# High less bias on GpSimd, and the low activations of the upper tiles straight from the bank

## The chip, the cores and the metric

The kernel runs on one core of a Trainium2 chip. A core has five engines that run side by side and wait for one another through semaphores: TensorE (matrix products, PE in the profile, with its weight loads as PEld), VectorE (DVE), ScalarE (ACT), GpSimd (POOL) and SyncE (SP), which here issues the loads. The metric is device time in microseconds, the median of several runs.

## The reference, cut to what matters

The program is two layers of a transformer-like trunk on 256 tokens of 1024 channels. Each layer has four sub-layers (gated feed-forward, a mixer of three branches, cross-attention, feed-forward), and each ends in a layer norm:

```
def layer_norm(x, g, b):
    mu = jnp.mean(xf, -1, keepdims=True)
    var = jnp.mean(jnp.square(xf - mu), -1, keepdims=True)
    return ((xf - mu) * lax.rsqrt(var + LN_EPS) * g + b)

for l in range(DEPTH):
    x = layer_norm(ALPHA * x + 0.5 * swiglu(x, ffn1_wg[l], ffn1_wu[l], ffn1_wd[l]), ln1_g[l], ln1_b[l])
    z = x @ w_in[l]
    ...
    x = layer_norm(ALPHA * x + merged @ mix_w_out[l], ln2_g[l], ln2_b[l])
    x = layer_norm(ALPHA * x + cross_attention(x, mem, xa_wq[l], xa_wkv[l], xa_wo[l]), ln3_g[l], ln3_b[l])
    x = layer_norm(ALPHA * x + 0.5 * swiglu(x, ffn2_wg[l], ffn2_wu[l], ffn2_wd[l]), ln4_g[l], ln4_b[l])
```

The result of each norm is the left operand of the next large product: `w_in` after norm 0, the queries after norm 1, the gate and up weights after norms 2 and 3. The last norm of the second layer is the output and does not go through the code that changes. So that code runs seven times.

## The kernel before, in words

**Products in parts.** TensorE works in float32r, which keeps fewer bits than float32. To hold the accuracy, each operand is split into a high part (rounded to float32r) and a low part (the exact value less the high part, rounded again). A product is then high x high, high x low and low x high.

**Weights.** SyncE loads pieces of 128x1024 into a ring of six (`ring_raw`). ScalarE copies a piece with rounding to `ring_hi`, a ring of three; VectorE subtracts, raw less high, to `ring_lo` (L1718, `lo_to`, 1024 columns a time). Three of the pieces in each layer are subtracted by GpSimd instead (L2444). A slot of `ring_hi` is free again when TensorE has multiplied the piece, so ScalarE, and behind it VectorE, follow TensorE.

**Activations.** `xT[0]` is the high part and `xT[1]` the low part of the normed activations, turned so that channels lie on the partitions: eight tiles of 128 channels x 256 tokens, numbered 0 to 7.

**A norm.** The norm sums up per token (L1732, L1737), GpSimd makes the inverse standard deviation (L2421), and the normed tokens are turned by TensorE into four banks (L850), two channel tiles to a bank. Banks 4 and 5 hold the lower tiles 0 to 3, banks 6 and 7 the upper tiles 4 to 7. What the turned values still need is the norm's gain and bias, which are one number for each channel and so for each partition here. From there two pairs of engines share the work:

- Lower tiles: ScalarE writes the high tiles (bank x gain + bias, rounded), then the same unrounded into `xf`. GpSimd subtracts (L2429), 128x512 at a time, two tiles of one bank.
- Upper tiles: VectorE does all of it. It writes four high tiles (L1755), then what the list `after` holds (in most norms one weight piece, L1718), then for each bank two unrounded tiles into `xf` (L1755 again) and one subtraction of 128x512 (L1769):

```
for b in range(2, 4):
    sl = slice(2 * b, 2 * b + 2)
    st.then(affine(xf, b))
    st.mark(tt(xT[1][:, sl, :], xf[:, sl, :], xT[0][:, sl, :], ALU.subtract), s_xTd)
```

`st.mark` raises a semaphore when the instruction is done; `st.then` also makes the engine wait for it. Each engine works in the order of its program. On VectorE the next work behind this code is the next weight piece. On GpSimd, behind the lower subtractions, norms 0 and 1 have passes of 128x1024 over `x_tok` (L2436, L2437), which scale the residual.

**The first product after a norm.** `first_chunk` takes two weight pieces m = 0 and m = 1. It first does all products of high activations, for m = 0 and then for m = 1 (L775, 32 of them), and then those of the low activations (L786, 16 of them, eight for each piece). Both go over the tiles in the order 4, 5, 6, 7, 0, 1, 2, 3. At L786 it waits for `s_xTd` before tiles 4 and 6 and for `s_xTp` (GpSimd's) before tiles 0 and 2. After norm 1 TensorE has other products to do ahead of `first_chunk`.

All waits in the region are written out by hand in the program; there is no planner.

Of the kernel before, what the change touches and what calls it, by code (L numbers as in the profile page):

```python
# [18 lines left out]
ALU = mybir.AluOpType  # L19
# [7 lines left out]
T = 256  # L27
# [137 lines left out]
def trunk(nc, io, consts, out):  # L165
    with ExitStack() as ctx:
# [17 lines left out]
        def sem(name, n=None):  # L184

            s = nc.alloc_semaphore(name)
            per_layer[s.name] = n
            return s

        def at(s, n):  # L190

            return s, layer[0] * per_layer[s.name] + n
# [19 lines left out]
        def view(region, at, *dims):  # L212

            n = 1
            for d in dims:
                n *= d
            v = region[:, at:at + n]
            if len(dims) == 1:
                return v
            names = "abcd"[:len(dims)]  # L220
            return v.rearrange(f"p ({' '.join(names)}) -> p {' '.join(names)}",
                               **{x: d for x, d in zip(names[1:], dims[1:])})
# [12 lines left out]
        def pc(name, k=0, n=1):  # L235
            a = (PCOL_A if name in PCOL_A else PCOL_B)[name][0]
            return pcol[:, a + k:a + k + n]

        xtok = view(xtok_t, 0, NT, D)
        xT = [view(xT_t, i * ND * T, ND, T) for i in range(2)]  # L240
# [64 lines left out]
        xf = view(work, 6144, ND, T)  # L305
# [44 lines left out]
        def bank(b, *dims):  # L350
            names = "abcd"[:len(dims)]
            if len(dims) <= 1:
                return banks[b][:, :]
            return banks[b][:, :].rearrange(f"p ({' '.join(names)}) -> p {' '.join(names)}",
                                            **{x: d for x, d in zip(names[1:], dims[1:])})
# [43 lines left out]
        s_xhd = sem("xT_hi_from_dve", 8)  # L399
        s_lnx = sem("ln_normalised_dve", 4)  # L400
        s_lnxa = sem("ln_normalised_act", 8)
        s_lnT = sem("ln_turned", 20)
        s_xTa = sem("xT_from_act", 8)
        s_xTd = sem("xT_from_dve", 8)
        s_xg = sem("x_tok_scaled_by_pool", 6)
        s_xgd = sem("x_tok_scaled_by_dve", 10)
# [187 lines left out]
        def done_chunk(eng, kind, j):  # L594

            eng.wait_ge(*at(s_piece, INDEX[(kind, j, 1)] + 1))
# [1107 lines left out]
        def _(dve):  # L1704
            st = Steps(dve, c_dve)
            v = nc.vector
            tt, ts, stt = v.tensor_tensor, v.tensor_scalar, v.scalar_tensor_tensor
# [13 lines left out]
            def ln(n, kind, j, scale, after, within=(), between=(), halfway=()):  # L1721

                if n in (1, 2):
                    dve.wait_ge(*at(s_xg, 4 * n - 2))
                for t in range(NT):
                    for h in range(2):
                        if t == 0 or h == 0:
                            dve.wait_ge(*at(s_acc, 3 * n + 2 * t + h + 1))
                        else:
                            done_chunk(dve, kind, j)  # L1730
                        x = xtok[:, t, 512 * h:512 * h + 512]
                        ins = stt(x, banks[4 + 2 * t + h][:, :], scale, x, ALU.mult, ALU.add)  # L1732
                        if h == 1:
                            st.then(ins, s_lny)
                        else:
                            st.then(ins)
                        st.then(v.bn_stats(stats[t][:, 6 * h:6 * h + 6], x))  # L1737
                    st.then(v.bn_aggr(mv[t], stats[t]))
                    st.mark(ts(vare[t], mv[t][:, 1:2], LNE, None, ALU.add), s_lnv)  # L1739
                    if t == 0:  # L1740
                        for piece in halfway:
                            lo_to(*piece, further=False)
                if n == 3 and layer[0] == L - 1:
                    return
                x = xtok[:, 1, 0:512]
                st.mark(ts(x, x, mv[1][:, 0:1], None, ALU.subtract), s_lnc)
                for piece in within:
                    lo_to(*piece, further=False)
                dve.wait_ge(*at(s_lnr, NT * n + NT))
                x = xtok[:, 1, 512:D]  # L1750
                st.mark(ts(x, x, mv[1][:, 0:1], rstd[1], ALU.subtract, ALU.mult), s_lnx)

                def affine(o, b):
                    for d in (2 * b, 2 * b + 1):
                        ins = ts(o[:, d, :], bank(4 + b, 2, T)[:, d % 2, :], pc(f"ln{n}_g", d), pc(f"ln{n}_b", d),  # L1755
                                 ALU.mult, ALU.add)
                    return ins

                for piece in between:
                    lo_to(*piece, further=False)  # L1760
                for b in range(2, 4):
                    dve.wait_ge(*at(s_lnT, 5 * n + b))
                    st.mark(affine(xT[0], b), s_xhd)
                for piece in after:
                    lo_to(*piece, further=False)
                for b in range(2, 4):
                    sl = slice(2 * b, 2 * b + 2)
                    st.then(affine(xf, b))
                    st.mark(tt(xT[1][:, sl, :], xf[:, sl, :], xT[0][:, sl, :], ALU.subtract), s_xTd)  # L1769

            def add_halves(kind, j, m, o):
                dve.wait_ge(*at(s_piece, INDEX[(kind, j, m)] + 1))
# [50 lines left out]
            for b in (2, 3, 0, 1):  # L1823
# [4 lines left out]
                sl = slice(2 * b, 2 * b + 2)  # L1828
# [193 lines left out]
            for l in range(L):  # L2022
# [81 lines left out]
                for t in range(NW):  # L2104
                    ins = ts(kk[:, t, :], zrw[:, 4 + t, 1:T + 1], pc("k_k", t), None, ALU.mult)
# [11 lines left out]
                for t in range(NW):  # L2117
                    ins = v.tensor_tensor_scan(dec[:, t, :], const("reset"), sw[:, t, :], 0.0, ALU.mult, ALU.add)
# [5 lines left out]
                for t in range(NW):  # L2124
                    ins = ts(rk[:, t, :], ra[:, t, :], pc("k_a", t), omka[:, t:t + 1], ALU.mult, ALU.add)
# [8 lines left out]
                for h in range(2):  # L2134
                    ins = tt(kk[:, 2 * h:2 * h + 2, :], kk[:, 2 * h:2 * h + 2, :], bank(4 + h, 2, T), ALU.mult)
# [16 lines left out]
                for t in range(NW):  # L2152
                    ins = tt(AR[:, t, :, 0, :], kk[:, t, :].rearrange("p (c s) -> p c s", c=NC),
                             eP[:, t, :].rearrange("p (c s) -> p c s", c=NC), ALU.mult)
                st.then(ins)
                dve.wait_ge(*at(s_exp, 3))
                for t in range(NW):
                    ins = tt(AR[:, t, :, 1, :], r_[:, t, :].rearrange("p (c s) -> p c s", c=NC),
                             eC[:, t, :].rearrange("p (c s) -> p c s", c=NC), ALU.mult)
# [3 lines left out]
                for h in range(2):  # L2163
                    ins = tt(bonus[:, 2 * h:2 * h + 2, :], bank(6 + h, 2, T), v_[:, 2 * h:2 * h + 2, :], ALU.mult)
# [140 lines left out]
                for h in range(2):  # L2305
                    ins = stt(yc[:, 2 * h:2 * h + 2, :], bank(4 + h, 2, T), -1.0 / C, yT[:, 2 * h:2 * h + 2, :],
                              ALU.mult, ALU.add)
# [7 lines left out]
                for t in range(NW):  # L2315
                    ins = ts(yc[:, t, :], yc[:, t, :], pc("gn_g", t), pc("gn_b", t), ALU.mult, ALU.add)
# [89 lines left out]
        def _(pool):  # L2406
            st = Steps(pool, c_pool)
            g = nc.gpsimd
            tt = g.tensor_tensor
# [4 lines left out]
            def ln(n, first=None):  # L2414

                final = n == 3 and layer[0] == L - 1
                if first:
                    piece_lo(*first)
                for t in range(NT):
                    pool.wait_ge(*at(s_lnv, NT * n + t + 1))  # L2420
                    st.then(tt(rstd[t], vare[t], NEG_HALF, ALU.pow), s_lnr)  # L2421
                    if t == 0:
                        st.mark(g.tensor_scalar(nbias[0], mv[0][:, 0:1], rstd[0], -1.0, ALU.mult, ALU.mult), s_lnb)
                if final:
                    return
                for b in range(2):
                    pool.wait_ge(*at(s_xTa, 2 * n + b + 1))
                    sl = slice(2 * b, 2 * b + 2)
                    st.mark(tt(xT[1][:, sl, :], xf[:, sl, :], xT[0][:, sl, :], ALU.subtract), s_xTp)  # L2429
                if n >= 2:  # L2430
                    return
                pool.wait_ge(*at(s_lnw, 32 * (n + 1)))
                pool.wait_ge(*at(s_xTd, 2 * n + 2))
                pool.wait_ge(*at(s_lnT, 5 * n + 5))
                for t in range(NT if n else 1):
                    st.then(tt(xtok[:, t, :], xtok[:, t, :], lnbc[:, 0, :], ALU.mult), s_xg)  # L2436
                    st.then(tt(xtok[:, t, :], xtok[:, t, :], lnbc[:, 1, :], ALU.add), s_xg)  # L2437
# [17 lines left out]
            for l in range(L):  # L2455
# [13 lines left out]
                for i in range(2):  # L2469
                    for h in range(2):  # L2470
                        ins = tt(c_bd[i][:, :, 64 * h:64 * h + 64], c_raw[i],
                                 half_c[:, h:h + 1].unsqueeze(2).to_broadcast([P, NW, C]), ALU.mult)
# [4 lines left out]
                for i in range(4):  # L2477
                    a, b = ((frb, fib), (fib, frb), (fr1b, fi1b), (fi1b, fr1b))[i]
# [3 lines left out]
                    for h in range(2):  # L2482
                        dst = b_bd[i].rearrange("p t (s h c) -> p (t s) h c", s=4, h=2)[:, :, h, :]
                        ins = tt(dst, bt_tmp[0], half_s[:, h:h + 1].unsqueeze(2).to_broadcast([P, NS, 16]), ALU.mult)
# [57 lines left out]
```

## Time and profile before

| | |
|---|---|
| time, median of 3 runs | 1641.42 us (1639.29 to 1641.63) |
| profiled execution: its time / its span | 1640.61 us / 1638.7 us |
| TensorE busy | 1589.4 us, 97% |
| VectorE busy | 1221.5 us, 75% |
| ScalarE busy | 757.0 us, 46% |
| GpSimd busy | 243.7 us, 15% |
| mean granted TensorE clock | 0.996 of full speed |

The span goes from the first to the last instruction of the profiled execution. Busy times are sums over the span; matmuls overlap one another in the records. What an engine waited for is told in the waits, the chain of waits and the timeline, where a bracket at the end of a row says how long the engine had been idle and what released it.

### The profile page before, as it was taken

To read this page: it belongs to the slowest core of one execution; us is meant where nothing else is said; L and a number is where in the kernel's file an instruction comes from. 1 tells how busy PE (TensorE), PEld (TensorE's weight loads), DVE (VectorE), ACT (ScalarE), POOL (GpSimd) and SP (SyncE) were. 2 spreads that over 40 slices of the span, in tenths; PEclk is the share of its full clock that TensorE was granted. 3 is DMA by queue.
4 is the path that set the end of the run, shared out by engine and by line. 5 is a ranking of instruction groups with operands and counts; after the bars stand their busy time and mean duration, and the time that the engine had idled before them with its cause. 6 is when DMAs were issued, how large, how long until landed. Compare 5 with 4: busy or idle time off the path is not lost.

```text
span 1638.7 us, 30659 instructions
## 1 busy us (share of the span) xinstructions
PE 1589.4 (97%) x12986; PEld 1415.1 (86%) x12986; DVE 1221.5 (75%) x1591; ACT 757.0 (46%) x969; POOL 243.7 (15%) x176
## 2 busy tenths in 40 slices
PE   8999989999999999999989999999999999989997
PEld 7788889989889897888878888899898889878886
DVE  5799899868456767766688998998674658486666
ACT  3554453653253554444455455346423535454443
POOL 1123620000000212101120335100000004020101
PEclk9999999999999999999999999999999999999999
DMA  7766655433436545666676656544334455456664
GB/s 204 232 184 182 203 142 143 130 116 107 139 110 202 163 131 168 188 188 192 204 193 191 193 179 181 156 142 128 105 109 140 127 195 167 146 157 186 192 187 134
DMA packets 380912, 267.70 MB, mean 163 GB/s; under 512 B 21132, under 2 KB 361576, under 8 KB 380776
## 3 DMA queue, kind: packets, MB, share of 16 engines
q1 hardware_dynamic: 377928, 255.25, 52.6%
q10 hardware_dynamic: 2848, 10.49, 1.9%
q8 instruction: 103, 1.69, 0.4%
q14 instruction: 33, 0.27, 0.1%
HBM read 264.66 MB, written 1.05 MB: 162 GB/s over the span
## 4 chain that ended last, share of the span: by engine, by line
PE 80%; DVE 14%; issue 3%; ACT 2%; DMA 1%; SPq 0%; POOL 0%; DVEq 0%; ACTq 0%
PE bank L740 17%; PE bank L743 9%; PE bank L732 7%; PE bank L719 6%; PE banks4to L721 6%; PE banks4to L719 6%; PE banks4to L720 6%; PE bank L720 6%; PE bank L721 6%; DVE ring_lo L1718 2%; DVE small L1737 1%; DVE x_tok L1732 1%; PE bank L786 1%; PE bank L1282 1%; PE bank L1266 1%
## 5 line engine op out<-in xcount | busy, mean ns | idle before, releaser
L1718 DVE TENSOR_TENSOR ring_lo<-ring_raw,ring_hi 128x1024 fp32r<-128x1024 f32 x438 | 568.6, 1302 | 230.8 <-ACT ring_hi L1327 226.4
L1327 ACT ACTIVATE ring_hi<-ring_raw 128x1024 fp32r<-128x1024 f32 x444 | 468.2, 1058 | 472.1 <-PE bank L743 198.9
L740 PE MATMUL bank<-xT,ring_hi 128*128 128x512 f32 x1344 | 335.8, 392 | 2.7 <-ACT ring_hi L1327 2.7
L740 PEld LDWEIGHTS bank<-xT,ring_hi 128*128 128x128 f32 x1344 | 244.3, 189 | 48.4 <-issue 3.3
L719 PE MATMUL bank<-xT,ring_hi 128*128 128x256 f32 x864 | 251.7, 291 | 2.9 <-DVE ring_lo L1718 2.6
L720 PE MATMUL bank<-xT,ring_hi 128*128 128x256 f32 x864 | 244.7, 283 | 0.0
L721 PE MATMUL bank<-xT,ring_lo 128*128 128x256 f32 x864 | 244.6, 283 | 0.0
L743 PEld LDWEIGHTS bank<-xT,ring_lo 128*128 128x128 f32 x1344 | 183.5, 191 | 13.0
L743 PE MATMUL bank<-xT,ring_lo 128*128 128x256 f32 x1344 | 187.5, 283 | 0.0
L719 PEld LDWEIGHTS bank<-xT,ring_hi 128*128 128x128 f32 x864 | 165.6, 192 | 9.1 <-issue 3.9
L720 PEld LDWEIGHTS bank<-xT,ring_hi 128*128 128x128 f32 x864 | 165.7, 192 | 0.6 <-issue 0.5
L721 PEld LDWEIGHTS bank<-xT,ring_lo 128*128 128x128 f32 x864 | 165.7, 192 | 0.0
L2450 POOL TENSOR_TENSOR hT_lo<-work,hT_hi 128x512 fp32r<-128x512 f32 x44 | 70.8, 1609 | 526.4 <-ACT hT_hi L1327 526.3
L719 PE MATMUL banks4to<-ring_hi,hT_hi 128*128 128x512 f32 x352 | 138.6, 394 | 2.3 <-DVE ring_lo L1718 2.3
L721 PE MATMUL banks4to<-ring_hi,hT_lo 128*128 128x512 f32 x352 | 139.7, 397 | 0.0
L720 PE MATMUL banks4to<-ring_lo,hT_hi 128*128 128x512 f32 x352 | 139.3, 396 | 0.0
L1774 DVE TENSOR_REDUCE work<-bank 128x256 f32<-128x512 f32 x176 | 116.9, 685 | 19.7 <-PE bank L743 19.3
L732 PE MATMUL bank<-region_z,ring_raw 128*128 128x256 f32 x384 | 87.7, 383 | 0.0
L2421 POOL TENSOR_TENSOR small<-small,constants 128x1 f32<-128x1 f32 x16 | 10.9, 681 | 495.8 <-DVE small L1739 495.8
L719 PEld LDWEIGHTS banks4to<-ring_hi,hT_hi 128*128 128x128 f32 x352 | 67.4, 191 | 18.3 <-issue 3.4
L732 PEld LDWEIGHTS bank<-region_z,ring_raw 128*128 128x128 f32 x384 | 71.6, 190 | 10.0
L721 PEld LDWEIGHTS banks4to<-ring_hi,hT_lo 128*128 128x128 f32 x352 | 66.1, 188 | 14.1
(317 smaller groups left out, 2330.8 us busy)
## 6 DMA issues: line engine op xcount, KB each, us to landing
ring_raw<-in_w_in_dram SPq DMA_DIRECT2D x100, 512.0 KB, 3.9
ring_raw<-in_ffn_wg_dram SPq DMA_DIRECT2D x88, 512.0 KB, 4.3
ring_raw<-in_ffn_wu_dram SPq DMA_DIRECT2D x88, 512.0 KB, 4.1
ring_raw<-in_ffn_wd_dram SPq DMA_DIRECT2D x88, 512.0 KB, 3.6
ring_raw<-in_xa_wkv_dram SPq DMA_DIRECT2D x32, 512.0 KB, 3.8
ring_raw<-in_s_glu_w_dram SPq DMA_DIRECT2D x16, 512.0 KB, 3.5
ring_raw<-in_mix_w_out_dram SPq DMA_DIRECT2D x16, 512.0 KB, 3.4
ring_raw<-in_xa_wq_dram SPq DMA_DIRECT2D x16, 512.0 KB, 4.0
```

Of the source, the lines that this page charges most:

```text
L719: mm(o, a[0], b[0], start=first, stop=False, **kw)
L720: mm(o, a[0], b[1], start=False, stop=False, **kw)
L721: return mm(o, a[1], b[0], start=False, stop=last, **kw)
L732: last = mm(o[:, c * T:(c + 1) * T], w[:, k, c * P:(c + 1) * P], src[:, k, :], start=(k == 0), stop=(k == NW - 1))
L740: mm(both, hi[:, k, :], xT_both[:, :, k, :], start=(k == 0), stop=(k == ND - 1), skip_group_check=True)
L743: last = mm(o[:, 0:T], lo[:, k, :], src[0][:, k, :], start=False, stop=(k == ND - 1), skip_group_check=True)
L786: last = mm(os[m][1], ws[m][0][:, k, :], xT[1][:, k, :], start=False, stop=(i == ND - 1), skip_group_check=True)
L1266: last = mm(o[:, t * M:(t + 1) * M], qT[:, 2 * h + d, t * P:(t + 1) * P], kmT[:, 2 * h + d, :], start=(d == 0), stop=(d == 1))
L1327: return nc.scalar.activation(o, i, func, **kw)
L1718: st.mark(tt(lo_flat(n), raw_flat(n), hi_flat(i), ALU.subtract), s_lo["dve"])
L1774: ins = v.tensor_reduce(o[:, m * T:(m + 1) * T], x.rearrange("p (a t) -> p t a", a=2), AX.X, ALU.add)
L2450: st.mark(tt(lo, htmp[j % 2], hi, ALU.subtract), s_hl)
```

## The change

Low is (bank x gain + bias) less high. The change writes it as bank x gain less (high less bias). VectorE computes this in one pass that reads the bank and `xf`, and `xf` now holds high less bias, which GpSimd makes from the high tiles. The unrounded copy of the upper tiles is no longer written. VectorE's pass is given out one tile at a time (128x256), since the gain is a column of its own for each tile. The same goes for GpSimd's.

```
+        s_xhb = sem("xT_hi_less_bias", 8)
...
@@ VectorE, ln(): in place of the loop quoted above
                 for b in range(2, 4):
-                    sl = slice(2 * b, 2 * b + 2)
-                    st.then(affine(xf, b))
-                    st.mark(tt(xT[1][:, sl, :], xf[:, sl, :], xT[0][:, sl, :], ALU.subtract), s_xTd)
+                    dve.wait_ge(*at(s_xhb, 2 * n + b - 1))
+                    for d in (2 * b, 2 * b + 1):
+                        ins = stt(xT[1][:, d, :], bank(4 + b, 2, T)[:, d % 2, :], pc(f"ln{n}_g", d), xf[:, d, :],
+                                  ALU.mult, ALU.subtract)
+                    st.mark(ins, s_xTd)
...
@@ GpSimd, ln(): ahead of the lower subtractions
                 if final:
                     return
+                for b in range(2, 4):
+                    pool.wait_ge(*at(s_xhd, 2 * n + b - 1))
+                    for d in (2 * b, 2 * b + 1):
+                        ins = g.tensor_scalar(xf[:, d, :], xT[0][:, d, :], pc(f"ln{n}_b", d), None, ALU.subtract)
+                    st.mark(ins, s_xhb)
                 for b in range(2):
                     pool.wait_ge(*at(s_xTa, 2 * n + b + 1))
```

The lower tiles, the high tiles, the weight splits and TensorE's program are as before.

## Rows read from the trace of the kernel before

**Rows 1.** The page, first part: busy us, share of the span, instructions.
```profile
PE 1589.4 (97%) x12986; PEld 1415.1 (86%) x12986; DVE 1221.5 (75%) x1591; ACT 757.0 (46%) x969; POOL 243.7 (15%) x176
```
**Rows 2.** Waits, whole span: total us, times, longest us.
```profile
PE bank L786 <- DVE xT L1769: 5.0, 5, 1.2
```
**Rows 3.** Chain of waits, 1436 to 1452 us: start us, us, what.
```profile
1441.60 1.90 DVE xT L1755 x4
...
1444.63 0.92 DVE work L1755 x2
...
1445.58 1.29 DVE xT L1769
1446.87 0.92 DVE work L1755 x2
...
1447.81 0.76 DVE xT L1769
...
1448.61 1.94 PE bank L786 x14
```
**Rows 4.** Timeline of VectorE, same stretch: start, us, engine, line, out and in.
```profile
1443.42 1.21 DVE L1718 TENSOR_TENSOR ring_lo<-ring_raw,ring_hi 128x1024 fp32r<-128x1024 f32 x1
...
1448.48 1.21 DVE L1718 TENSOR_TENSOR ring_lo<-ring_raw,ring_hi 128x1024 fp32r<-128x1024 f32 x1
```
**Rows 5.** Timeline of GpSimd, same stretch.
```profile
1445.02 2.99 POOL L2429 TENSOR_TENSOR xT<-work,xT 128x512 fp32r<-128x512 f32 x2 [4.53 <-ACT work L1327]
```
**Rows 6.** Timeline of TensorE, same stretch.
```profile
1442.74 0.36 PE L775 MATMUL bank<-xT,ring_hi 128*128 128x256 f32 x1 [0.53 <-DVE xT L1755]
...
1445.08 0.28 PE L775 MATMUL bank<-xT,ring_hi 128*128 128x256 f32 x1
...
1447.00 0.43 PE L786 MATMUL bank<-xT,ring_hi 128*128 128x256 f32 x2
```
**Rows 7.** Timeline of ScalarE, same stretch.
```profile
1443.84 1.94 ACT L1327 ACTIVATE work<-banks4to,param_columns 128x256 f32<-128x256 f32 x4
1445.64 1.10 ACT L1327 ACTIVATE ring_hi<-ring_raw 128x1024 fp32r<-128x1024 f32 x1
```
**Rows 8.** One line, L2429, same stretch: duration ns min/median/max.
```profile
L2429 POOL TENSOR_TENSOR xT<-work,xT x2: 1301/1519/1737, 1445.0 to 1446.3; 128x512 fp32r<-128x512 f32 x2
```
**Rows 9.** Timeline of GpSimd and VectorE, 185 to 190 us.
```profile
185.52 1.29 POOL L2494 TENSOR_TENSOR region_r<-work 128x512 f32<-128x512 f32 x1
185.65 2.24 DVE L1718 TENSOR_TENSOR ring_lo<-ring_raw,ring_hi 128x1024 fp32r<-128x1024 f32 x1 [1.11 <-ACT ring_hi L1327]
...
186.90 2.35 POOL L2495 TENSOR_SCALAR region_r<-region_r 128x512 f32<-128x512 f32 x1
...
189.02 1.21 DVE L1718 TENSOR_TENSOR ring_lo<-ring_raw,ring_hi 128x1024 fp32r<-128x1024 f32 x1
```
**Rows 10.** Three lines, whole span: duration ns min/median/max.
```profile
L2423 POOL TENSOR_SCALAR small<-small x8: 264/265/949, 204.3 to 1628.7; 128x1 f32<-128x1 f32 x8
L2481 POOL TENSOR_TENSOR work<-work x8: 732/1334/1807, 119.1 to 976.3; 128x256 f32<-128x256 f32 x8
L2061 DVE SCALAR_TENSOR_TENSOR region_z<-region_z,param_columns,bank x8: 480/482/482, 263.6 to 1116.8; 128x256 f32<-128x256 f32 x8
```
**Rows 11.** Timeline of VectorE and TensorE at norm 1, 566 to 572 us.
```profile
566.75 4.56 DVE L1718 TENSOR_TENSOR ring_lo<-ring_raw,ring_hi 128x1024 fp32r<-128x1024 f32 x2
...
570.04 2.08 PE L786 MATMUL bank<-xT,ring_hi 128*128 128x256 f32 x16
```
**Rows 12.** Window of TensorE (busy, clock, DMA share, GB/s), and timeline.
```profile
632.00:634.00 2.00, 2.00 (x10) 0.50 0.00 0
...
639.55 1.93 PE L786 MATMUL bank<-xT,ring_hi 128*128 128x256 f32 x14 [0.22 <-DVE xT L1769]
```
**Rows 13.** Timeline of GpSimd and VectorE at norm 0, 1028 to 1035 us.
```profile
1028.83 3.28 POOL L2437 TENSOR_TENSOR x_tok<-x_tok,work 128x1024 f32<-128x1024 f32 x1
...
1033.22 1.23 DVE L2067 TENSOR_TENSOR x_tok<-x_tok,work 128x1024 f32<-128x1024 f32 x1
```

## The prediction

> **What bounds the kernel now.** The first part of the page: TensorE is busy 97% of the span, VectorE 75%, GpSimd 15% [rows 1]. So VectorE or GpSimd time is worth something only where TensorE waits for it. The waits over the whole span come next: TensorE waits for the line that the change replaces, the low activations of the upper tiles, 5.0 us in 5 waits, the longest 1.2 [rows 2]. That is the whole prize, 0.30% of the span.
>
> Seven norms run this code (n = 0 to 3 in the first layer, 0 to 2 in the second). The chain of waits through the last of them says how the wait arises [rows 3]. VectorE makes the four high tiles (1441.60 to 1443.50), splits a weight piece [rows 4], and then goes for each of two banks through an unrounded copy (two passes, 0.92) and a subtraction (1.29, then 0.76). TensorE has done its high products by then, does the first two low ones at 1447.00 [rows 6], and resumes at 1448.61 with fourteen in a row.
>
> Off that chain, GpSimd makes the low activations of the lower tiles, bank by bank, from 1445.02 to 1448.00 [rows 5]. TensorE takes the tiles in the order 4, 5, 6, 7, 0, 1, 2, 3, so tiles 2 and 3 are wanted four products after the resume (0.12 apart: fourteen in 1.94, the last one 0.28 long), at 1449.09. GpSimd beats that by 1.1 us. If VectorE were instant, they would be wanted at 1447.00 + 0.72 = 1447.7, so GpSimd is already the next to be late, by 0.4.
>
> **The change, part by part.** All in the norm at 1442, then carried to the others.
>
> *VectorE.* Per bank two copies and a subtraction (0.92 + 1.29 and 0.92 + 0.76, 3.9 in all) become two passes that read the bank and one tensor. The nearest row is a pass of the same kind, with a bank among its inputs, 0.48 for 128x256 [rows 10]; so about 1.0 a bank and 2.0 in all. VectorE saves 1.9 us in each norm, if its inputs are there.
>
> *GpSimd, added.* Four passes of 128x256, high less bias, ahead of its two subtractions. The trace has this operation only at other sizes: 128x1 takes 0.26 [rows 10], 128x512 takes 2.35 [rows 9]. That 2.35 holds a wait. In the same rows a VectorE split that began at 185.65, just after a GpSimd pass (185.52 to 186.81), took 2.24 in place of 1.21: it stood until the GpSimd pass was over. The GpSimd pass of 186.90 then stood until that split ended at 187.89, so its own work is 189.25 - 187.8 = 1.44. The two engines take turns, a whole instruction at a time, when VectorE reads two tensors from SBUF. A subtraction of 128x512 takes 1.29 there and one of 128x256 0.73 [rows 9, 10], so I scale 1.44 by 0.73 / 1.29 to 0.8 for one new pass. Bounds: 0.26 below (the tiny one), 1.17 above (half of 2.35, as if nothing in it were a wait). Half of 1.44 is 0.72.
>
> The Trainium skill says otherwise. Its GPSIMD Engine Reference (4.1, Engine selection) calls GpSimd roughly line-rate for one input, which by its clock of 1.2 GHz would make 256 elements some 0.2 us beside the start-up, about 0.4 together as an estimate; the 1.44 above for 512 speaks against it. What it would give is the first rival below.
>
> *The sum on GpSimd, pass 0.8.* It can begin when TensorE does, at the end of the second high tile, 1442.7 (TensorE at 1442.74) [rows 6]. Pass 1: to 1443.5. VectorE's split comes at 1443.42 [rows 4], gets the turn and holds it to 1444.5; passes 2, 3 and 4 then end at 1445.3, 1446.1 and 1447.0. The subtraction for the first lower bank, whose input ScalarE has had ready since about 1444.9 [rows 7], used to begin at 1445.02; now it runs 1447.05 to 1448.35 (1.30 when undisturbed [rows 8]).
>
> *VectorE behind its new waits.* Bank one: 1445.3 to 1446.3. Bank two waits for pass 4, so 1447.0 to 1448.05; before, it was ready at 1448.57, so this part is 0.5 earlier. Queued behind these waits is the next weight split, which began at 1448.48 [rows 4]. It now comes at about 1448.1, and its rounded part was there by 1446.74 [rows 7]. That is inside GpSimd's first subtraction, so it takes the turn when that one is over: 1448.2 to 1449.3. The second subtraction stands until then and needs 1.2 more, which is what the disturbed one of the pair shows today (1.74 long, freed when VectorE's subtraction ended at 1446.87) [rows 3, 8]. Tiles 2 and 3 are ready at 1450.5, TensorE goes on at 1450.55 in place of 1449.09: 1.45 us late. The wait for VectorE is gone, and a longer one for GpSimd is in its place.
>
> The skill's SBUF — State Buffer (Who interferes with whom) has a VectorE instruction with at most one SBUF input outside the turn-taking. So the new VectorE pass should not be blocked. If it were, the second bank would stand behind GpSimd's first subtraction, the weight split would come after the second one, and the loss would be 0.6 and not 1.45.
>
> *The other norms.* Four of the seven look alike, each with a wait of 1.18: 4 x 1.45 = 5.8. The one at 632 has TensorE at half clock, 0.50 [rows 12], so its high products end late and its wait is 0.22. There GpSimd would begin at 633.2 and end 7.75 later, TensorE goes on at 641.05 against 639.55 + 0.48: 1.0 late. In the two at n = 1, TensorE still has memory products to do and takes its first low one at 570.04 [rows 11]; GpSimd would be through by 569.3. The cost is in the weight split at 566.75 (piece wanted at 568.0): it meets GpSimd's first subtraction and ends about 0.2 later, 0.4 for both. The four long x_tok passes behind it on GpSimd move by 2.3, with their consumer far away. At n = 0 two such passes follow, and VectorE waits for them. The last ended at 1032.11, while VectorE was busy with its own pair up to 1034.45 [rows 13]. Both sides slip together with TensorE by about 1.4, so nothing is added. A first split at 1443.42 that has to wait for pass 1 ends by 1444.7, wanted at 1445.08 [rows 6]: free.
>
> Sum: 5.8 + 1.0 + 0.4 = 7.2 us. The profiled execution took 1640.61 (span 1638.7, the rest around it); 1640.61 + 7.2 = 1647.8, and the median of the runs is 0.8 above the profiled one, so I say 1648. Three of the four passes count in full, so with 0.72 per pass a norm loses 1.2 and the sum is 6.0; with 0.86 (a straight line through 0.26 and 1.44) it is 8.1; with the upper bound 1.17 a norm loses 2.55, 12.8 in all and a time of 1654.
>
> **The rivals.**
> *The GpSimd pass is short, about 0.4.* Passes 1 to 4 end by 1445.5, the second VectorE bank is ready at 1446.65, GpSimd is through at 1448.05, and TensorE takes tiles 2 and 3 at 1448.15: 0.94 earlier, four times, and 0.2 at the norm at 632. That is 4.0 off, 1637.4. For it: the skill's rule, and that the only 128x512 row is an indirect reading. Against it: that reading comes from a row that repeats in both layers, and the subtractions scale as I took them. It can't pass the 5.0 of rows 2. Chance 0.13.
> *The second subtraction keeps its place ahead of the split.* The split reaches GpSimd's first subtraction only some 0.15 before its end. If the two new VectorE passes take 1.2 together and not 1.0, the subtraction pair runs through and ends at 1449.6: 0.6 late, four times, and 0.1: 2.5 in all, 1644, which is no measurable change. So is a pass of 0.6: GpSimd's second pass starts before the split, all shifts forward, and the norms lose 0.65 or less. Chance 0.27 together.
> *The clock.* TensorE ran at half clock around 632 [rows 12], in the norm where its waits just before are like those of the others. The new waits between the low products add up to 2.8 us. If the clock fell in one of them, the 24 products behind it would take up to twice their 0.12 each, 2 to 3 us more: 1650 to 1652. Only 0.05 of the chance, inside the slower cases.
>
> **How the numbers follow.** The forecast with its own spread (1645 to 1651) and the clock's case hold 0.60. Faster than the median by over 0.2% (3.3 us, which is what a measurement of this kernel can tell) needs the first rival nearly in full: 0.12. Within 0.2%: 0.28. Slower: 0.60. The range reaches down through the second rival and part of the first to 1639, and up to 1652 for a longer pass.
>
> **What the profile will show.** TensorE's waits at L786 should be some 0.6 us for VectorE before tile 6 and, before tile 2, about 1.8 for the GpSimd subtraction (L2429 before), in the norms that wait 1.18 now. The new GpSimd pass should be 0.7 to 0.9 undisturbed, its second about 1.8 long in the list because of the split. The pair of lower subtractions should start 2.0 later than now and its second member should take about 2.2. VectorE should stand idle ahead of its new passes. If TensorE's longest wait there still names VectorE, or the new pass is 0.4, I am wrong.

## The result and the profile after

The changed kernel takes 1652.38 us (median; 1650.45 to 1652.98, 4 runs) against 1641.53 before: a ratio of 1.0069, 95% interval 1.0057 to 1.0081. Measured once more beside later kernels it took 1654.6, a ratio of 1.0083 (1.0070 to 1.0097). It is slower, as forecast, but by 11 to 14 us and not by 6.5, and just outside the range of 1639 to 1652.

The first part of the page of the changed kernel answers to [rows 1]. VectorE is 14 us less busy, GpSimd 32 us more, and TensorE's share is the same:

```profile
PE 1597.3 (97%) x12986; PEld 1420.0 (86%) x12986; DVE 1207.1 (73%) x1577; ACT 757.6 (46%) x969; POOL 276.1 (17%) x204
```

The waits of the changed kernel over the whole span (total us, times, longest) answer to [rows 2]. What was 5.0 us for VectorE is 2.5, and 8.5 for GpSimd has come beside it:

```profile
PE bank L787 <- POOL xT L2437: 8.5, 5, 1.7
...
PE bank L787 <- DVE xT L1770: 2.5, 4, 0.8
```

The timelines of the last norm, which starts at 1452.36 here and at 1441.60 in [rows 3], for VectorE, GpSimd and TensorE in that order (start, us, engine, line, out and in; L1770 is the pass over the bank, L2432 the new GpSimd pass, L2437 the lower subtraction, L1719 the weight split, L787 the low products):

```profile
1454.17 1.22 DVE L1719 TENSOR_TENSOR ring_lo<-ring_raw,ring_hi 128x1024 fp32r<-128x1024 f32 x1
1456.21 0.88 DVE L1770 SCALAR_TENSOR_TENSOR xT<-banks4to,param_columns,work 128x256 fp32r<-128x256 f32 x2 [0.83 <-POOL work L2432]
1458.02 0.88 DVE L1770 SCALAR_TENSOR_TENSOR xT<-banks4to,param_columns,work 128x256 fp32r<-128x256 f32 x2 [0.92 <-POOL work L2432]
1458.81 1.48 DVE L1719 TENSOR_TENSOR ring_lo<-ring_raw,ring_hi 128x1024 fp32r<-128x1024 f32 x1
```
```profile
1453.52 4.46 POOL L2432 TENSOR_SCALAR work<-xT,param_columns 128x256 f32<-128x256 f32 x4 [2.28 <-DVE xT L1756]
1457.95 3.46 POOL L2437 TENSOR_TENSOR xT<-work,xT 128x512 fp32r<-128x512 f32 x2
```
```profile
1458.95 0.82 PE L787 MATMUL bank<-xT,ring_hi 128*128 128x256 f32 x4 [0.78 <-DVE xT L1770]
1461.47 1.45 PE L787 MATMUL bank<-xT,ring_hi 128*128 128x256 f32 x10 [1.70 <-POOL xT L2437]
```

The reader is to see the new order: four GpSimd passes take 4.46 us, so the lower subtractions start at 1457.95, 5.6 us into the norm in place of 3.4. VectorE stands idle ahead of each of its two banks. TensorE waits a little for VectorE and then 1.70 for GpSimd.

Durations of the two GpSimd lines, the new pass over the whole span and the two subtractions of this norm (ns min/median/max):

```profile
L2432 POOL TENSOR_SCALAR work<-xT,param_columns x28: 915/927/1750, 209.7 to 1457.1; 128x256 f32<-128x256 f32 x28
```
```profile
L2437 POOL TENSOR_TENSOR xT<-work,xT x2: 1260/1749/2238, 1458.0 to 1459.2; 128x512 fp32r<-128x512 f32 x2
```

Against the pair in [rows 8], the second one has grown from 1.74 to 2.24: the weight split of 1458.81 has its turn in front of it.

One more thing differs. Windows of TensorE just behind two of the norms in the changed kernel (busy, granted clock, DMA share, GB/s) show half clock (1.2 of 2.4 GHz). The third row is the kernel before behind the first of them, at full clock, as behind its other four:

```profile
218.00:220.00 2.00, 2.00 (x15) 0.50 0.18 43
...
1037.00:1039.00 2.00, 2.00 (x70) 0.54 0.69 186
```
```profile
217.00:221.00 4.00, 4.00 (x93) 1.00 0.80 227
```

In the profiled execution this happens behind four of the five norms in which TensorE waits, each time for 3.4 us. It doesn't happen behind the fifth, the norm shown above, after the same waits of 0.78 and 1.70.

Not all half clock lies there. A second kind of stretch begins at the start of a norm, between 2 us before its first high tile and 2 us after, so that the high products run at half clock. The kernel before has one (6.8 us from 630.4, [rows 12]), the changed kernel two (from 634.4 and from 828.9). One window of the changed kernel and then two of e14_fill, a kernel described below:

```profile
829.00:832.00 3.00, 3.00 (x15) 0.50 0.14 38
```
```profile
828.00:831.00 3.00, 2.92 (x14) 0.50 0.01 2
1449.50:1452.50 3.00, 3.00 (x15) 0.50 0.02 5
```

Every version measured here has one to three stretches of this second kind in its profile, and each has one more at the very end of the program. The experiments on the clock are about the first kind.

To compare kernels, I use one length: from the start of the first high tile to the end of the last low product of the first chunk. In the norm above that is 1462.92 - 1452.36 = 10.56. In the kernel before it is 1450.55 - 1441.60 = 8.95.

| kernel | a norm with a wait, full clock | after norm 1 | time, us | ratio to before (95%) |
|---|---|---|---|---|
| before | 8.93 | 11.75 | 1641.5 | |
| changed | 10.56 | 12.12 | 1652.4 | 1.0069 (1.0057 to 1.0081) |
| e1_fill | 10.57 | 14.7 | 1655.0 | 1.0090 (1.0076 to 1.0104) |
| e2_hold | 9.6 | 17.2 | 1659.7 | 1.0116 (1.0102 to 1.0130) |
| e3_vector | 9.07 | 13.28 | 1645.1 | 1.0028 (1.0018 to 1.0038) |
| e5_nobias | 7.48 | 11.6 | 1638.5 | 0.9983 (0.9974 to 0.9992) |
| e6_one_pass | 8.17 | 11.6 | 1639.9 | 0.9995 (0.9986 to 1.0003) |
| e7_fill | 10.57 | 12.11 | 1648.7 | 1.0048 (1.0035 to 1.0062) |
| e8_hold | 9.6 | 12.12 | 1646.8 | 1.0039 (1.0026 to 1.0051) |
| e9_mixed | 7.95 | 12.63 | 1640.0 | 0.9995 (0.9986 to 1.0003) |
| e10_before_fill | 9.38 | 11.74 | 1644.4 | 1.0025 (1.0016 to 1.0034) |
| e11_both | 7.95 | 11.61 | 1639.7 | 0.9995 (0.9986 to 1.0004) |
| e12_tt_each | 9.45 (norm 0: 8.46) | 11.6 | 1643.3 | 1.0015 (1.0007 to 1.0024) |
| e13_after | none at full clock: 10.73 to 11.62 | 12.12 | 1654.6 | 1.0083 (1.0070 to 1.0097) |
| e14_fill | 10.58 | 12.11 | 1649.4 | 1.0053 (1.0039 to 1.0067) |

Half clock inside a norm can lengthen it beyond this column: 9.36 in the kernel before (its norm at 632), 11.3 to 11.6 in the three kernels that add fillers to the changed one, 8.88 in e5_nobias. In e12_tt_each the norms of 9.45 have half clock in their high products, but TensorE still waits for GpSimd behind them, so GpSimd sets their length.

### The profile page after: what moved, and what is told of

Same layout as the page of the kernel before. It is cut to its first block and busy times, and to the rows that moved or that the text cites. A ratio compares the mean times of both kernels' runs of the same rounds, so it can differ in the third digit from the quotient of the medians.

```text
span 1651.1 us, 30673 instructions
## 1 busy us (share of the span) xinstructions
PE 1597.3 (97%) x12986; PEld 1420.0 (86%) x12986; DVE 1207.1 (73%) x1577; ACT 757.6 (46%) x969; POOL 276.1 (17%) x204
## 3 DMA queue, kind: packets, MB, share of 16 engines
q8 instruction: 103, 1.69, 0.4%
## 5 line engine op out<-in xcount | busy, mean ns | idle before, releaser
L1719 DVE TENSOR_TENSOR ring_lo<-ring_raw,ring_hi 128x1024 fp32r<-128x1024 f32 x438 | 565.7, 1295 | 242.0 <-ACT ring_hi L1328 237.7
```

Source lines behind the costliest of these rows:

```text
L1719: st.mark(tt(lo_flat(n), raw_flat(n), hi_flat(i), ALU.subtract), s_lo["dve"])
```

## The experiments

My theory at the start: GpSimd's chain is late by 1.6 us a norm (first by the size of its passes, then by a turn that the weight split takes in the middle), and half clock follows the longer wait. The rivals were that the clock falls by itself, that the passes' size doesn't matter, and that the gain on VectorE was never worth anything.

### The clock: fillers in TensorE's waits

```
+ for _ in range({6: 2, 2: 4}.get(k, 0)):
+     mm(os[m][1], ident, ZERO.to_broadcast([P, T]), start=False, stop=False, skip_group_check=True)
  pe.wait_ge(... s_xTp or s_xTd ...)
```

A filler is a product of the unit matrix with zeros. It adds nothing to the bank, and TensorE has something to do while it would wait: two fillers ahead of tile 6, four ahead of tile 2.

> The changed kernel with six idle-time products of TensorE added in each first chunk (two ahead of the wait for tile 6, four ahead of the wait for tile 2; each adds zeros to the bank and takes about 0.4 us), so that TensorE works while it waits. Theory 1, the clock: of the 10.9 us lost, about 5 come from TensorE being granted half clock for 3.4 us after the new waits (four times in the profiled execution of the changed kernel, at 218, 645, 839 and 1037 us). Then these four falls go and the time is 1646 to 1648.5, with tile 2 still about 1.6 us late in each of five norms. Rival: the falls come where they will and have nothing to do with the waits; then the time stays at 1651 or above and as many half-clock stretches are seen.

Measured 1655.0: slower than the changed kernel, and my forecast missed, because of the experiment's own design. After norm 1 TensorE has no wait, so the six fillers simply added 2.6 us there, twice. Norms with a wait kept 10.57 at full clock, and no half clock was left just behind any of the five. Two stretches of the second kind remained (from 830.7 and from 1451.9). So it was run again without fillers after norm 1 (`if n != 1 else 0`).

> As e1_fill, but without the six filler products after norm 1, where TensorE has no wait to fill: in e1_fill they made each of those two first chunks 2.6 us longer, 5.2 us in all, while the five norms with waits kept the length of the changed kernel (10.57 us from the first high tile to the last low product). Theory 1 (half clock follows the new waits): 1655.0 less 5.2, so 1649 to 1650.5, some 2.5 us under the changed kernel, and no half-clock stretch within 2 us behind a first chunk. Rival (clock falls independent of the waits): 1651.5 to 1653.

1648.7, a little better than forecast (1649 to 1650.5). But it was compared with the changed kernel only through two ratios whose intervals touch. Both kernels were therefore run once more on one chip in one session.

> The changed kernel once more, unedited, side by side with the filled one on the same chip, since the two were so far only compared through the kernel before, whose two ratios (1.0069 and 1.0048) have touching intervals. If the clock's share is real, this one is again 10.5 to 12 us over the kernel before, and 2.5 to 4.5 us over the filled one.

> The kernel of e7_fill once more, unedited (fillers of TensorE in its waits, none after norm 1). Theory (half clock behind the new waits costs 3 to 4 us): 7 to 8.5 us over the kernel before and clearly under e13_after. Rival (the two are the same and 3.4 us was the chip's or the hour's difference): within 1 us of e13_after.

1654.6 (1653.8 to 1655.2) against 1649.4 (1647.6 to 1651.6): 5.2 us apart, with no overlap. The direction is as forecast, the sizes are not quite: e13_after is 13.9 over the kernel before (10.5 to 12 forecast), e14_fill 8.7 (7 to 8.5), and the distance was to be 2.5 to 4.5. Windows of TensorE behind the norms, first of e13_after, then of e14_fill:

```profile
218.00:220.00 2.00, 2.00 (x10) 0.50 0.09 26
...
645.00:647.00 2.00, 2.00 (x8) 0.50 0.78 232
...
840.00:842.00 2.00, 2.00 (x8) 0.50 0.63 189
...
1037.00:1039.00 2.00, 2.00 (x70) 0.50 0.56 149
...
1465.00:1467.00 2.00, 2.00 (x7) 0.55 1.05 304
```
```profile
217.00:221.00 4.00, 4.00 (x89) 1.00 0.42 118
644.00:648.00 4.00, 4.00 (x23) 1.00 1.03 273
839.00:843.00 4.00, 4.00 (x27) 1.00 0.89 243
1036.00:1040.00 4.00, 4.00 (x35) 1.00 0.84 214
1461.00:1465.00 4.00, 4.00 (x27) 1.00 0.99 285
```

The column after the instruction count is the granted clock. Without fillers it is half behind all five norms, with them it is full behind all five (and full behind all five in the profiles of e1_fill and e7_fill). What TensorE did before each of these falls was to stand for 0.4 to 0.8 and then for 1.70 us within 3, or in one norm for 1.69 alone, after high products at half clock. So the half clock behind the norms comes from the waits, and the rival is out for it. Stretches of the second kind are there without fillers and with them (three in the profile of e13_after, two in that of e14_fill); what sets them off is not shown.

The price of one stretch follows. The end of the program left out, the profiled executions took 1655.24 with eight stretches and 1649.10 with two: 6.1 us for six, about 1.0 each. The 5.2 of the medians can be a little too low as the price of the waits' half clock. Where the high products of e14_fill run at half clock, there is no idle time left behind them that could hide it, and those two norms take 11.48 and 11.33, where the like norms of the changed kernel took 10.86 and 10.71.

The control fills the wait of the kernel before:

```
+ for _ in range({6: 3, 2: 1}.get(k, 0) if n != 1 else 0):
+     mm(os[m][1], ident, ZERO.to_broadcast([P, T]), start=False, stop=False, skip_group_check=True)
```

> The kernel before with filler products of TensorE in its own wait (three ahead of the wait for tile 6, one ahead of tile 2, none after norm 1). The control for the clock: the kernel before waits 1.18 us there and shows no half-clock stretch behind it, so filling that wait should bring nothing, 1640.5 to 1642.5, and the fillers may cost up to 0.4 us a norm. Rival: waits of this length already cost clock in most executions of the kernel before, and the changed kernel's loss to the clock is not its own; then this one is over 2 us faster, under 1639.

1644.4, above the forecast of 1640.5 to 1642.5. The fillers didn't fit the wait: a norm took 9.38 in place of 8.93, which is 2.3 of the 3.7 us; where the rest went is not shown. It is far from the rival's 1639, and there is full clock behind all five norms in the profile of the kernel before as well as in this one. So the four waits of 1.18 brought none, and what the changed kernel loses to it is its own. As a control by time it is weak, since the fillers cost something; the profiles carry the point.

### Taking turns: VectorE holds its split back

```
+ dve.wait_ge(*at(s_xTp, 2 * n + 2))      # behind the two banks
```

> The changed kernel with one more wait on VectorE: it holds its next weight split back until GpSimd has done both lower subtractions. Theory 2, taking turns: GpSimd's second lower subtraction takes 2.2 us in the changed kernel because that split takes its turn in front of it. Then the second one takes 1.3, tile 2 is ready about 1.0 earlier, TensorE's wait before it is 0.7 and not 1.7, the clock falls less often, and the time is 1643 to 1648. Rival: GpSimd's subtraction is slow for another reason (its own work, or the four passes in front of it); then its second subtraction stays at 2.2 and the time moves by less than 1 us, or rises by the later split.

Measured 1659.7, where 1643 to 1648 was forecast. The norms with a wait went to 9.6, but after norm 1 the held split is the one that TensorE needs next, and that cost 5 us twice (17.2). Run again with `if n != 1` ahead of it:

> As e2_hold, but VectorE holds its split back only in the five norms where TensorE waits, not after norm 1 (there the held split cost 5 us each time). Theory 2 (the split takes its turn ahead of GpSimd's second lower subtraction): the five norms take 9.6 us and not 10.57, so 4.5 to 5 us less than the changed kernel, and a wait of 0.73 in place of 1.70 is short enough for fewer clock falls: 1645 to 1648. Rival (what the hold wins in the norm the late split gives back after it): 1651 to 1654.

1646.8, inside the forecast. The two subtractions at the norm that starts near 1022 in e8_hold now take 2.50 together in place of 3.46, and TensorE's total wait for them fell from 8.5 to 3.2. First the timeline of GpSimd there, then the waits:

```profile
1027.55 2.50 POOL L2439 TENSOR_TENSOR xT<-work,xT 128x512 fp32r<-128x512 f32 x2
```
```profile
PE bank L787 <- POOL xT L2439: 3.2, 5, 0.7
```

So one turn of the split, in the wrong place, costs 0.97 us a norm. The clock is better too: with a last wait of 0.73, half clock follows one of the five norms (from 217.5, on waits of 0.78 and 0.73), where it followed four and five in the two profiles of the changed kernel. Its share of the time was not measured by itself.

### Size and kind of the GpSimd pass

One pass a bank, the bias spread as a second tensor:

```
- for d in (2 * b, 2 * b + 1):
-     ins = g.tensor_scalar(xf[:, d, :], xT[0][:, d, :], pc(f"ln{n}_b", d), None, ALU.subtract)
- st.mark(ins, s_xhb)
+ sl = slice(2 * b, 2 * b + 2)
+ bias = pc(f"ln{n}_b", 2 * b, 2).unsqueeze(2).to_broadcast([P, 2, T])
+ st.mark(tt(xf[:, sl, :], xT[0][:, sl, :], bias, ALU.subtract), s_xhb)
```

> The changed kernel with GpSimd's high less bias as one pass of 128x512 for each bank, the bias spread over the tokens as a second input, in place of two passes of 128x256 (0.92 each undisturbed). My step on size: the loss scales with what GpSimd has in front of its lower subtractions. Such a pass with a spread input took 1.04 to 1.3 for 128x512, so GpSimd is through about 1 us earlier, the five norms take 9.5 to 9.9, and the time is 1645 to 1648.5. Rival: the size of these passes does not matter, since the turns with VectorE set the end; then 1651 or more.

1639.9: the whole loss is gone, far more than I forecast (12.5 us under the changed kernel). The pass takes 1.04 undisturbed, the norm 8.17:

```profile
L2433 POOL TENSOR_TENSOR work<-xT,param_columns x14: 1039/1531/2027, 209.6 to 1442.2; 128x512 f32<-128x512 f32 x14
```

I had missed a threshold. GpSimd's first lower subtraction starts 4.1 us into the norm, its second 5.4. The weight split comes only later, because ScalarE has the rounded part ready no earlier: 6.3 us in after norm 0, and 5.5 to 5.6 us in at the other three, when the second subtraction is already running. The split no longer gets its turn between the two (they take 2.53 to 2.56 together). TensorE's wait is 0.43 at most, and no half clock follows any of the five norms. Three costs go with one edit.

To tell kind from number, the same with four passes of 128x256:

```
- ins = g.tensor_scalar(xf[:, d, :], xT[0][:, d, :], pc(f"ln{n}_b", d), None, ALU.subtract)
+ ins = tt(xf[:, d, :], xT[0][:, d, :], pc(f"ln{n}_b", d).to_broadcast([P, T]), ALU.subtract)
```

> The changed kernel with its four GpSimd passes of 128x256 kept as four, but each with the bias spread over the tokens as a second input in place of a scalar column. In e6_one_pass two such passes of 128x512 (1.04 us undisturbed) took the whole loss away; two things changed there, the kind of the operation and the number of instructions. Theory (kind): the pass with a scalar column is the slow one, 0.92 for 256 columns against 0.6 for the spread one; the four take 2.5 undisturbed and not 3.7, GpSimd is through 1 to 1.3 earlier, the norms take 9.2 to 9.7 us against 10.57 and 8.17, and the time is 1643 to 1647. Rival (number): what costs is one more instruction and one more turn with VectorE; then the norms stay above 10.2 and the time at 1649 or above.

1643.3, as forecast for kind (1643 to 1647). The pass takes 0.61 where the one with a scalar column takes 0.92 (the line of the new pass and TensorE's wait for GpSimd in e12_tt_each):

```profile
L2432 POOL TENSOR_TENSOR work<-xT,param_columns x28: 608/612/1596, 209.0 to 1447.6; 128x256 f32<-128x256 f32 x28
```
```profile
PE bank L787 <- POOL xT L2437: 4.0, 5, 1.3
```

The norm takes 8.46 after norm 0, where the split comes late, and 9.45 in the others, where it takes its turn: 1.0 apart, the same price as in e8_hold, within one kernel. The two lower subtractions take 2.54 together after norm 0 and 3.52 to 3.55 in the others.

### What the VectorE part is worth alone

The low part is made without the bias, straight from the high tile, and GpSimd's passes are left out:

```
- ins = stt(xT[1][:, d, :], bank(...), pc(f"ln{n}_g", d), xf[:, d, :], ...)
+ ins = stt(xT[1][:, d, :], bank(...), pc(f"ln{n}_g", d), xT[0][:, d, :], ...)
```

> The change's VectorE part alone: the low part is bank x gain less high, with the bias left out of it (so the low activations of the upper tiles are off by the bias), in one VectorE pass for each tile, and no GpSimd pass at all. My theory: what VectorE gives is real (two us earlier), and what is next late is GpSimd's lower subtraction, 0.3 to 0.4 us a norm; so 0.8 to 0.9 us is gained in four norms, and the time is 1637 to 1638.5 against 1641.5 before. Rival: the wait for VectorE was hidden or is given back later in the layer (weight splits); then the time is that of before, 1640.5 to 1642.

1638.5, at the upper end of the forecast. TensorE has no wait for low tiles left (7.48), which is more than I forecast: without VectorE's subtraction in between, the two lower ones of GpSimd run through undisturbed. Yet of 1.45 a norm, seven or so in all, only 2.2 us reach the time. After norm 0 about 1.0 is given back each time: from the end of the first chunk to the next norm's first high tile it is 342.76 us before and 343.79 here. TensorE is through sooner and then waits for a weight split right behind the chunk:

```profile
218.65 0.36 PE L720 MATMUL bank<-xT,ring_hi 128*128 128x256 f32 x1 [1.40 <-DVE ring_lo L1719]
```

In the profile, part of the rest went to half clock in the high products: one of the five norms took 8.88 and one 7.91.

### Where else high less bias can be made

On VectorE alone, with GpSimd's new passes and the wait for them taken out:

```
+ for d in (2 * b, 2 * b + 1):
+     ins = ts(xf[:, d, :], xT[0][:, d, :], pc(f"ln{n}_b", d), None, ALU.subtract)
+ st.then(ins, s_xhb)
```

> Everything on VectorE: high less bias is made by VectorE too (four passes of 128x256 from SBUF to SBUF, 0.35 to 0.4 each by similar rows), followed by the pass over the bank; GpSimd does what it did before. Theory: VectorE needs 0.7 + 0.9 a bank and not 0.92 + 1.29 or 0.76, ready for tile 6 about 0.6 us earlier than before, GpSimd's lower subtractions as early as before, no new wait; time 1638.5 to 1640.5, faster than both. Rival: the passes from SBUF to SBUF take turns with GpSimd's two lower subtractions and stand up to 1.2 us each; then 1641 to 1645, still below the changed kernel.

1645.1: the forecast of 1638.5 to 1640.5 missed, and the rival (1641 to 1645) was right. These passes take turns with GpSimd too, up to 1.41 us each, and after norm 1 the weight split behind them comes 1.4 late for TensorE (the line's durations, then TensorE's waits for the split in the first chunk, in e3_vector):

```profile
L1770 DVE TENSOR_SCALAR work<-xT,param_columns x28: 343/416/1407, 210.8 to 1449.9; 128x256 f32<-128x256 f32 x28
```
```profile
PE bank L776 <- DVE ring_lo L1719: 2.8, 2, 1.4
```

The Trainium skill's SBUF — State Buffer (Who interferes with whom) counts tensor_scalar, the operation of these passes, among those that can enter a mode in which they contend with GpSimd. The 1407 ns agree. The passes over the bank, which read one tensor from SBUF, never went above 485 ns in the changed kernel, GpSimd busy or not.

Tiles 4 and 5 on VectorE, 6 and 7 on ScalarE:

```
+ act.wait_ge(*at(s_xhd, 2 * n + 2))      # ScalarE, behind its unrounded lower tiles
+ for d in (6, 7):
+     ins = f(xf[:, d, :], xT[0][:, d, :], ACT.Identity, scale=-1.0, bias=pc(f"ln{n}_b", d))
+ st.mark(ins, s_xfu)
...                                        # VectorE: its own passes for tiles 4 and 5, and an add for 6 and 7
```

> No pass on GpSimd: VectorE makes high less bias itself for tiles 4 and 5 (0.61 for both when undisturbed, as seen in e3_vector), ScalarE makes bias less high for tiles 6 and 7 behind its unrounded lower tiles, and VectorE adds that to bank x gain. In e3_vector the second pair of passes stood 1.4 us behind GpSimd's second lower subtraction; here there is none to stand. Theory: tile 6 is ready 0.9 us earlier than in the kernel before, the norms take 8.0 to 8.2 us against 8.93; part is given back after norm 0, where VectorE is the later engine (in e5_nobias 1.0 of 1.45 was); 1638 to 1640.5, faster than both. Rival: ScalarE's two more passes delay the next weight piece by 1 us and the gain goes there; then 1641 to 1643.

1640.0, inside the forecast. The norms came out at 7.95 (8.0 to 8.2 forecast), after norm 1 it lost 0.9. And the best of both (one GpSimd pass a bank at norm 1, e9_mixed's form in the others):

```
+ for b in range(2, 4) if n == 1 else ():           # GpSimd; ScalarE returns early at n == 1
...
+     st.mark(tt(xf[:, sl, :], xT[0][:, sl, :], bias, ALU.subtract), s_xb1)
```

> The two good forms together: after norm 1, where TensorE has no wait, GpSimd makes high less bias in one pass a bank (11.60 us there in e6_one_pass against 12.63 in e9_mixed), and in the other norms VectorE and ScalarE make it (7.95 in e9_mixed against 8.17). By these lengths 1.8 us less than e9_mixed: 1638 to 1639, some 0.15% under the kernel before. Rival: VectorE's later work takes it back as it did after norm 0; then 1639.5 to 1640.5, the same as before.

1639.7: no gain over e9_mixed that can be measured, so the time is the rival's (1639.5 to 1640.5) and not the forecast's. After norm 1 it did come down, to 11.61. In its profile the three norms after norm 1 (at 632, 824 and 1441) had half clock in their high products and took 8.75 to 8.94, where the profile of e9_mixed has one such norm (8.72). Whether that is what took the gain back is not shown. No version that keeps the bias beats the kernel before by more than the measurement can tell; e6_one_pass, e9_mixed and e11_both are all within 0.1% of it. (e5_nobias, which leaves the bias out, is 0.17% under it.)

## Why the prediction was right and where it failed

**What bounds it, and the order of events: right.** The wait for VectorE shrank to 0.78 before tile 6 (I had 0.6), and one of 1.70 for the GpSimd subtraction took the place before tile 2 (I had 1.8). The second new pass is 1.75 long because of the split, the second subtraction 2.24 (I had 2.2). e8_hold and e12_tt_each show the turn of the split by itself: 1.0 us.

**The size of the new pass: too small.** "So I scale 1.44 by 0.73 / 1.29 to 0.8 for one new pass." It is 0.92. The 1.44 was a product with a constant for 512 elements, and I scaled it by how passes with two tensors shrink; the new pass, which takes its number from a column, doesn't follow that. (With the split's end as the row has it, 187.89, the 1.44 would even be 1.36.) Three such passes are on the path, less some slack: a norm lost 1.64 and not 1.45. The straight line through 0.26 and 1.44, which I had as a bound, gave 0.86, also low.

**The sum, point by point.** Norms at full clock, measured: 5 x 1.64 = 8.2, with 6.8 forecast. The one at 632 is counted like the others here; in the kernel before, half clock had lengthened it by 0.4 (9.36). After norm 1: 0.37 twice, 0.7, with 0.4 forecast. "Both sides slip together with TensorE by about 1.4, so nothing is added" was wrong in sign: something is given back. In the kernel before, TensorE waits 0.94 for a weight split 28 us after norm 0; in the changed one 0.17 (timelines of TensorE, before and after):

```profile
245.93 0.36 PE L719 MATMUL bank<-xT,ring_hi 128*128 128x256 f32 x1 [0.94 <-DVE ring_lo L1718]
```
```profile
247.96 0.36 PE L720 MATMUL bank<-xT,ring_hi 128*128 128x256 f32 x1 [0.17 <-DVE ring_lo L1719]
```

That is 0.77 back, and the same again in the second layer: -1.5. In e5_nobias and e9_mixed TensorE waits for a split 1.40 and 1.10 right behind this first chunk instead: behind norm 0 VectorE sets the pace, so what TensorE wins there is lost again. 8.2 + 0.7 - 1.5 = 7.4. The two kernels with fillers, which have all of this and no half clock behind the norms, measured 7.8 and 8.7 over the kernel before. The profile of the second accounts for the difference: its two norms with half clock in the high products are 1.7 longer together, less the 0.4 of the kernel before, so 8.7. (The same count gives 9.6 for the profiled execution of the first, its slowest, which was 10.9 over; 1.3 of that stays open.) So the sum without the clock was nearly right (7.2), with its pass too small and its give-back missing, which cancel by luck. Two slips: 1647.8 + 0.8 is 1648.6 and not 1648, and with VectorE instant GpSimd would be late by 0.3 (1448.00 less 1447.72) and not by 0.4. And my own upper bound for the pass gave 1654, while the range ends at 1652.

**The clock: the step that failed.** The sum has no term for the clock. It stands only as a rival: "If the clock fell in one of them [...] 2 to 3 us more: 1650 to 1652. Only 0.05 of the chance." It fell behind four of five norms in one profile and all five in the other, and the waits' half clock costs 3.4 us by the ratios of the changed kernel and e7_fill and 5.2 by e13_after against e14_fill. The number of falls was wrong, and so was the price of one: about 1.0, where I had 2 to 3. (The new waits, too, add up to 0.6 + 1.8 = 2.4 by my own figures and not to 2.8; 2.5 was measured.) What I had right is the way it works. The row that I read, half clock around 632, came after waits of 1.8 and 1.2 us ahead of the norm; the norms at 824 and 1441 have waits like these and kept full clock in that profile. That was a sign that one profile doesn't say how often the clock falls, and that a new wait of 1.7 in every norm could bring more of it. 7.4 + 3.4 to 5.2 is 10.8 to 12.6, and with the 1.3 for half clock in the high products, as above, 13.9 for the second pair; 10.9 and 13.9 were measured. How many stretches an execution without a profile has is not known, so this last step rests on two profiles.

**The rivals.** A pass of 0.4 was not there. The subtraction that keeps its place did not come in the changed kernel, but e6_one_pass is just that case: no turn in between, and the time of before. The passes of 0.61 in e12_tt_each are the rival's pass of 0.6: 1643.3, where I had put this case at 1644 at most.

## What to carry to other kernels

When work moves to an idle engine, add up that engine's own chain to the moment its last result is wanted: GpSimd was 15% busy and still became the bound, because its existing work there was 1.1 us from being late. On GpSimd, give a column operand as a spread tensor and make one pass of it (1.04 for 128x512) rather than two passes with a scalar column (0.92 each). Where TensorE already stands several times in a row, price a longer wait with the half clock behind it (about 1 us a stretch here), and test by filling the wait.

## What the runs showed of the hardware

- On GpSimd a subtraction of a scalar column takes 0.915 us for 128x256; the same with the column spread as a second tensor takes 0.608, and 1.039 for 128x512.
- GpSimd and VectorE take turns between instructions when VectorE reads two tensors from SBUF: a 128x1024 split got in between two back-to-back GpSimd subtractions and made the second 2.24 us long in place of 1.26.
- VectorE passes from SBUF to SBUF with one tensor input, 0.343 undisturbed, stood up to 1.41 behind GpSimd; passes with a bank and one SBUF tensor stayed at 0.47 to 0.49 throughout.
- TensorE fell to half clock for 3.4 us after waits of 1.7 us, with a shorter one close ahead in all but one case, in 9 of 10 norms of the two profiles of the changed kernel, and in none of 10 (e7_fill, e14_fill) when the waits were filled with products. Each such stretch cost about 1.0 us. Behind the four waits of 1.18 us in the kernel before there was none.
- Half clock in the high products, at the start of a norm, came with the fillers as well as without them: one to three stretches in every profile. What sets off one of these was not tested.
